# Layer c of a chain of eight layers: gate and output products in half-K pieces among heads and attention, squares on ScalarE with sums on VectorE, probabilities turned unscaled

## The chip, the core and the metric

One NeuronCore of a Trainium2 chip runs the whole program. The metric is the device time of one execution in microseconds. TensorE, VectorE, ScalarE, GpSimd and SyncE each work through their own instructions in order and meet at semaphores.

## What is computed

`x` (1 x 256 x 1024, float32) goes through eight residual layers: two of differential attention (a0, a1), a gated convolution (b), a latent attention (c), a window attention with a convolution (h), a dense feed-forward (ffn), a recurrent layer (r) and a mixture of experts (moe), in the order a0, b, c, a1, h, ffn, r, moe. The change is in c:

```python
def _mla(h, w_in, cq_g, w_uq, ckv_g, w_ukv, q_g, k_g, w_out):
    proj = h @ w_in
    c_q, c_kv, k_rope, gate = jnp.split(proj, [256, 384, 448], axis=-1)
    q = (_rms_norm(c_q, cq_g) @ w_uq).reshape(bsz, seq, 8, 192)
    kv = (_rms_norm(c_kv, ckv_g) @ w_ukv).reshape(bsz, seq, 8, 256)
    ...
    q_nope = _rms_norm(q_nope, q_g[:128])
    q_rope = _apply_rope(_rms_norm(q_rope, q_g[128:]), cos, sin)
    k_nope = _rms_norm(k_nope, k_g[:128])
    ...
    s = (qn @ kn.T + qr @ k_rope.T) * scale
    p = _chunk_causal_softmax(s, s0)
    o = p @ v
    ...
    return (o * jax.nn.silu(gate)) @ w_out
```

## The kernel before, in words

Tokens lie in two tiles of 128. Every weight matrix comes as granules of up to 128 x 2048 floats (1 MB). Each granule is split into two parts for TensorE: ScalarE writes the high part (`split`, L847), then VectorE the low part (L850), and a product is three matmuls a chunk (`three_passes`, L883 to L885). There are six raw slots and three split slots, so granule n is split only when n - 3 has been used. Where ScalarE and VectorE do this is decided by `ahead`: before a step of the order it emits the splits of all granules whose slot was used by an earlier step. A split is thus an instruction in the queue, with everything behind it waiting.

Eight PSUM banks are given out when the program is built (`plan_banks`): a ring of four short-lived ones (0 to 3) and one of four long-lived ones (4 to 7), each in the order of the steps. A step that needs a bank waits until its last user is released (semaphores `freed_0` to `freed_7`; `filled_n` is the other direction).

Layer c runs in three stages, in the order that `c_order` and `attention_order` give to all engines. *Gate stage*: low ranks of both tiles ("low"), four gate products ("gate"), and the turned low ranks ("lowturn"). *Head stage*: for each pair of heads and tile a q product (two heads of 192 columns) and a kv product (two heads of 256), ScalarE's squares with the accumulator (L2107), the inverse root on GpSimd (`inverse_root`, L1110, L1111: add eps, power), scaling and rotation by VectorE (L2186, `rope_one` L2212 to L2217 for q; L2198 for k), and transposes back (qturn, kturn), which ScalarE copies. An item is one such q or kv of one tile; there are 16. *Attention*: 16 steps (tile, head): scores, maximum (L1369), exponential (L1322), reciprocal and scaling of the probabilities (L1382, L1386), transposes ("weights", L1275), values (L1289), product with the gate (L1399), transposes ("output", L1298). Then the output product (`out_tensor`), the sum into x (L1218) and x's transposes for the next layer (`turn_x`, L1004).

The order of the head stage before:

```python
    for pair in range(5):
        for kind in ("q", "kv"):
            if pair < 4:
                order += [(kind, 2 * pair), (kind, 2 * pair + 1)]
            if pair >= 1:
                order += [("qturn" if kind == "q" else "kturn", i) for i in (2 * pair - 2, 2 * pair - 1)]
```

## Time and profile before

| | |
|---|---|
| median of 3 runs | 2138.75 us (2137.68 to 2139.63) |
| the profiled execution | 2138.28 us |
| its span, first to last instruction | 2136.5 us |
| TensorE busy | 1989.5 us (93%) |
| VectorE, ScalarE, GpSimd busy | 1588.1, 1236.1, 143.5 us |
| mean granted TensorE clock | 0.968 of 2.4 GHz |
| layer c, from its gate products to the next layer's first product | 346.2 to 479.3 us |

Times in rows are microseconds from the span's start, unless a mean is in ns. DVE is VectorE, ACT ScalarE, PE TensorE's matmuls, PEld its weight loads, POOL GpSimd. "idle before <-releaser" says how long the engine stood and what ended it. The clock is a share of 2.4 GHz, 0.5 being 1.2 GHz. Ends of matmuls are modelled and overlap the next start.

### The profile page before, as it was taken

The numbers are of one execution on the slowest core, as the hardware profiler recorded it, in microseconds if no ns is written. First come the engines' busy times: TensorE is split into PE (matmuls) and PEld (weight loads), VectorE is DVE, ScalarE is ACT, GpSimd is POOL, SyncE is SP. The second block draws the span as 40 slices with busy tenths as digits, with TensorE's granted clock in tenths as the row PEclk, the third lists the DMA queues.
The fourth block names the chain that finished last, engine by engine and source line by source line (L and its number), as shares of the span: only waits on it lengthen the run. The fifth ranks groups of instructions, "written<-read, shape, count | busy, mean of one in ns | idle before, by whom it ended". The sixth has DMA issues, their size and how long they took to land.

```text
span 2136.5 us, 26626 instructions
## 1 busy us (share of the span) xinstructions
PE 1989.5 (93%) x9460; PEld 1654.3 (77%) x9460; DVE 1588.1 (74%) x1962; ACT 1236.1 (58%) x1494; POOL 143.5 (7%) x209
## 2 busy tenths in 40 slices
PE   7988989689988799999889999999999999999998
PEld 6767868467867578887877878888888888888886
DVE  6664975558556744444678888898888889888887
ACT  5451135535554344343567767777777777777775
POOL 3013401305001000000000000000000000000000
PEclk9999999699999789999999999999999999999999
DMA  8422234205324225555147989899898989989894
GB/s 321 142 79 82 103 127 168 77 25 195 128 71 150 86 101 195 184 190 190 48 197 278 373 311 373 341 367 371 334 367 336 374 341 365 376 332 374 322 375 191
DMA packets 70518, 499.98 MB, mean 234 GB/s; under 512 B 8736, under 2 KB 8736, under 8 KB 10528
## 3 DMA queue, kind: packets, MB, share of 16 engines
q1 hardware_dynamic: 70432, 498.87, 62.4%
q8 instruction: 50, 0.82, 0.2%
q14 instruction: 36, 0.29, 0.0%
HBM read 497.79 MB, written 1.05 MB: 233 GB/s over the span
## 4 chain that ended last, share of the span: by engine, by line
PE 81%; DVE 10%; ACT 4%; issue 3%; POOL 1%; DMA 0%; DVEq 0%; SPq 0%; ACTq 0%; POOLq 0%
PE psum L883 24%; PE psum L885 23%; PE psum L884 23%; PE psum L1882 4%; DVE low L850 3%; ACT high L847 2%; PE psum L2850 2%; PE psum L2911 1%; PE psum L1890 1%; POOL small L1111 1%; PE psum L1127 1%; ACT h L1616 1%; DVE x L1218 0%; PE psum L1898 0%; DVE small L1659 0%
## 5 line engine op out<-in xcount | busy, mean ns | idle before, releaser
L850 DVE TENSOR_TENSOR low<-raw,high 128x2048 fp32r<-128x2048 f32 (+1 forms) x460 | 1046.6, 2281 | 307.2 <-ACT high L847 304.4
L847 ACT ACTIVATE high<-raw 128x2048 fp32r<-128x2048 f32 (+1 forms) x460 | 877.3, 1912 | 418.8 <-PE psum L885 395.7
L883 PE MATMUL psum<-high,yT_high 128*128 128x512 f32 x1672 | 669.6, 400 | 52.6 <-DVEq L2190 16.9
L885 PE MATMUL psum<-high,yT_low 128*128 128x512 f32 x1672 | 659.0, 394 | 0.0
L884 PE MATMUL psum<-low,yT_high 128*128 128x512 f32 x1672 | 657.5, 393 | 0.0
L883 PEld LDWEIGHTS psum<-high,yT_high 128*128 128x128 f32 x1672 | 318.6, 191 | 127.2 <-issue 37.2
L885 PEld LDWEIGHTS psum<-high,yT_low 128*128 128x128 f32 x1672 | 318.7, 191 | 68.1
L884 PEld LDWEIGHTS psum<-low,yT_high 128*128 128x128 f32 x1672 | 319.7, 191 | 62.0
L883 PE MATMUL psum<-high,hT_high 128*128 128x512 f32 (+2 forms) x560 | 220.2, 393 | 13.4 <-DVE h L1793 6.1
L885 PE MATMUL psum<-high,hT_low 128*128 128x512 f32 (+2 forms) x560 | 216.3, 386 | 0.0
L884 PE MATMUL psum<-low,hT_high 128*128 128x512 f32 (+2 forms) x560 | 216.1, 386 | 0.0
L883 PEld LDWEIGHTS psum<-high,hT_high 128*128 128x128 f32 x560 | 105.3, 188 | 38.6 <-issue 11.0
L885 PEld LDWEIGHTS psum<-high,hT_low 128*128 128x128 f32 x560 | 105.2, 188 | 21.3
L884 PEld LDWEIGHTS psum<-low,hT_high 128*128 128x128 f32 x560 | 105.4, 188 | 19.9
L1882 PE MATMUL psum<-arena,raw 128*128 128x256 f32 x384 | 83.7, 379 | 0.0
L1882 PEld LDWEIGHTS psum<-arena,raw 128*128 128x128 f32 x384 | 72.9, 190 | 9.9
L1971 DVE SCALAR_TENSOR_TENSOR arena<-arena,const 128x256 f32<-128x256 f32 x184 | 74.5, 481 | 0.4
L883 PE MATMUL psum<-hT_high,high 128*128 128x256 f32 x224 | 64.8, 290 | 4.9 <-DVE low L850 3.6
L884 PE MATMUL psum<-hT_low,high 128*128 128x256 f32 x224 | 64.0, 286 | 0.0
L885 PE MATMUL psum<-hT_high,low 128*128 128x256 f32 x224 | 64.0, 286 | 0.0
L2963 ACT ACTIVATE arena<-psum 128x512 f32<-128x512 f32 x56 | 33.5, 599 | 45.5 <-PE psum L885 45.5
L1917 ACT ACTIVATE arena<-psum,const 128x256 f32<-128x256 f32 x16 | 6.7, 470 | 78.9 <-PE psum L1882 78.9
(326 smaller groups left out, 1775.5 us busy)
## 6 DMA issues: line engine op xcount, KB each, us to landing
raw<-in_moe_weights SPq DMA_DIRECT2D x336, 1024.0 KB, 4.8
raw<-in_weights SPq DMA_DIRECT2D x132, 1024.0 KB, 5.0
raw<-in_weights SPq DMA_DIRECT2D x2, 896.0 KB, 4.6
raw<-in_weights SPq DMA_DIRECT2D x2, 768.0 KB, 4.4
x<-in_x SPq DMA_DIRECT2D x2, 512.0 KB, 4.2
raw<-in_weights SPq DMA_DIRECT2D x2, 512.0 KB, 3.6
out_x<-x SPq DMA_DIRECT2D x1, 1024.0 KB, 5.6
const<-in_constants SPq DMA_DIRECT2D x1, 512.0 KB, 8.4
```

Of the source, the lines that this page charges most:

```text
L847: eng.activation(high, raw, ACT.Copy).then_inc(k.high_ready, 1)
L850: eng.tensor_tensor(low, raw, high.bitcast(F32), ALU.subtract).then_inc(k.low_ready, 1)
L883: pe.matmul(out, lhs.high, rhs.high, start=start, stop=False)
L884: pe.matmul(out, lhs.high, rhs.low, start=False, stop=False)
L885: return pe.matmul(out, lhs.low, rhs.high, start=False, stop=stop)
L1111: pool.tensor_tensor(rstd, rstd, k.neghalf[:, 0:n], ALU.pow).then_inc(ready, 1)
L1127: last = pe.transpose(k.bank(("norm", n, i))[:, first:first + P], k.h[:, t, P * c:P * (c + 1)], k.ident)
L1616: last = act.activation(probs[:, s % 2, SEQ * m:SEQ * m + e], k.bank(name)[:, SEQ * m:SEQ * m + e], ACT.Exp, bias=low[:, m:m + 1], scale=q ...
L1882: last = pe.matmul(k.bank(name)[:, SEQ * half:SEQ * (half + 1)], w[:, c, P * half:P * (half + 1)], b.hT[:, c, :], start=(c == 0), stop=(c ...
L1971: last = v.scalar_tensor_tensor(b.conv[:, c, :], window, weight, b.conv[:, c, :], ALU.mult, ALU.add)
L2850: last = pe.matmul(k.bank(name)[:, P * (c % 4):P * (c % 4 + 1)], k.h[:, tile, P * c:P * (c + 1)], b.placed[:, tile, :], start=(tile == 0), ...
L2963: k.release(act.activation(b.silu[:, i % 2, :], k.bank(name), ACT.Silu), name)
```

## The change

All of it is in layer c. `c_order` is now written out, with eight half-K pieces of the gate product (unit, half, tile) between head products and transposes; pieces take long-lived banks. kv products come first. Squares of q and kv are plain ScalarE operations into a buffer, and VectorE sums them (`reduce`), one item ahead of the scaling (`C_REDUCE_LEAD = 1`). The rotation of q runs over both heads at once, with the root applied after it. Buffers of q and k are four deep. The attention has its own functions: probabilities are transposed unscaled, the reciprocal of the sums goes into the product of values and gate, and the output product too comes in eight half-K pieces, at steps 11, 13, 15, 19 and 20, the last three after step 22.

```diff
+    return [
+        ("low", 0), ("low", 1), gate(0, 0, 0), gate(0, 0, 1), ("lowturn", 0), ("lowturn", 1), gate(0, 1, 0),
+        ("kv", 0), ("kv", 1), ("q", 0), ("q", 1), gate(0, 1, 1), ("kv", 2), ("kv", 3), ("kturn", 0), ("kturn", 1),
+        ("q", 2), ("q", 3), gate(1, 0, 0), ("qturn", 0), ("qturn", 1), ("kv", 4), ("kv", 5), ("kturn", 2), ("kturn", 3),
...
+C_TURN_LAG, C_VALUE_LAG, C_REDUCE_LEAD = 2, 4, 1
+C_PIECES = {
+    11: [(0, 0, 0)], 13: [(1, 0, 0)], 15: [(0, 1, 0)], 19: [(0, 0, 1)], 20: [(1, 0, 1)], C_STEPS - 1: [(1, 1, 0), (0, 1, 1)],
+}
...
+    return order + [("turn_x", 0), ("turn_x", 1), ("piece", ("out", 1, 1, 1))]
...
-            for m, (first, n) in enumerate(parts):
-                last = act.activation(b.junk[:, junk:junk + n], bank[:, first:first + n],
-                                      ACT.Square, scale=float(n) ** -0.5, accum_out=k.group_ms[:, col + m:col + m + 1])
...
+                act.activation(squares[:, 0:2 * C_NOPE].rearrange("p (h n) -> p h n", h=2), heads[:, :, 0:C_NOPE], ACT.Square,
+                               scale=float(C_NOPE) ** -0.5)
...
+    def reduce(n):
+        kind, i = turns[n]
+        ahead(k, v, ("c", kind, i))
+        v.wait_ge(k.c_squares, n - 1)
+        last = v.tensor_reduce(k.group_ms[:, col:col + 2], squares[:, 0:2 * C_NOPE].rearrange("p (h n) -> p h n", h=2), AX, ALU.add)
...
+    for n in range(2, len(turns) + C_REDUCE_LEAD):
+        if n < len(turns):
+            reduce(n)
+        if n - C_REDUCE_LEAD >= 2:
+            at = n - C_REDUCE_LEAD
+            {"q": consume_q, "kv": consume_kv}[turns[at][0]](at)
...
+            steps.link(v.reciprocal(k.out_rstd[:, place:place + GROUP], k.c_sums[:, GROUP * g:GROUP * (g + 1)]))
+            for h in range(GROUP):
+                last = v.scalar_tensor_tensor(b.y[:, g % 2, cols], k.bank(name)[:, cols], k.out_rstd[:, place + h:place + h + 1],
+                                              b.gate[:, t, 512 * half + C_V * h:512 * half + C_V * (h + 1)], ALU.mult, ALU.mult)
...
+    ahead(k, v, k.banks.ticks[("c", C_STEPS - 1)])
+    add_to_x(k, v, ("c", "out", 2), 0, 1)
+    add_to_x(k, v, ("c", "out", 1), 1, 0)
```

The first place is VectorE's queue in the middle of the head stage. Before, from a split over kv 2 and kv 3 (`arena<-psum`, L2198) to the first head of q 4:

```order
L850 TENSOR_TENSOR low<-raw,high 128x2048 [waits dve_own,high_ready]
L2198 SCALAR_TENSOR_TENSOR arena<-psum,small,spread 128x128 [waits c_v_ready,filled_2,group_rstd_ready]
L2198 SCALAR_TENSOR_TENSOR arena<-psum,small,spread 128x128
L2198 SCALAR_TENSOR_TENSOR arena<-psum,small,spread 128x128 [waits freed_0,c_v_ready,filled_3,group_rstd_ready]
L2198 SCALAR_TENSOR_TENSOR arena<-psum,small,spread 128x128
L2186 SCALAR_TENSOR_TENSOR h<-psum,small,spread 128x128 [waits freed_1,filled_2,group_rstd_ready]
L2212 SCALAR_TENSOR_TENSOR h<-psum,small,arena 128x64
L2213 SCALAR_TENSOR_TENSOR h<-psum,small,arena 128x32
L2214 SCALAR_TENSOR_TENSOR h<-psum,small,arena 128x32
L2217 TENSOR_TENSOR h<-h 128x64 [waits dve_own]
L2186 SCALAR_TENSOR_TENSOR h<-psum,small,spread 128x128 [waits dve_own]
```

Now, from the sum of kv 7's squares (L2323) over the scaling of kv 6 (L2384), two splits (L907), the sums of q 4 (L2323, L2325) and the scaling of kv 7 to the sums of q 5:

```order
L2323 TENSOR_REDUCE small<-arena 128x2 [waits freed_1,c_squares]
L2384 SCALAR_TENSOR_TENSOR arena<-psum,small,spread 128x128 [waits group_rstd_ready,c_v_ready,filled_2]
L2384 SCALAR_TENSOR_TENSOR arena<-psum,small,spread 128x128
L907 TENSOR_TENSOR low<-raw,high 128x2048 [waits freed_0,high_ready]
L907 TENSOR_TENSOR low<-raw,high 128x2048 [waits high_ready]
L2323 TENSOR_REDUCE small<-arena 128x2 [waits c_squares]
L2325 TENSOR_REDUCE small<-arena 128x2
L2384 SCALAR_TENSOR_TENSOR arena<-psum,small,spread 128x128 [waits group_rstd_ready,c_v_ready,filled_3]
L2384 SCALAR_TENSOR_TENSOR arena<-psum,small,spread 128x128
L2323 TENSOR_REDUCE small<-arena 128x2 [waits freed_1,c_squares]
L2325 TENSOR_REDUCE small<-arena 128x2
```

Sums stand between the scalings, each waits for ScalarE's squares (`c_squares`), and two splits stand ahead of q 4's.

The second place is TensorE's queue at the same stage. Before, the transposes of kv 0 and kv 1 (L2075), and the product of q 4 to the first matmul of q 5's:

```order
L2075 MATMUL psum<-const,arena 128x128 [waits freed_2,c_k_staged]
L2075 MATMUL psum<-const,arena 128x128
L2075 MATMUL psum<-const,arena 128x128 [waits freed_3,c_k_staged]
L2075 MATMUL psum<-const,arena 128x128
L883 MATMUL psum<-high,yT_high 128x384 [waits low_ready,freed_0,freed_1]
L884 MATMUL psum<-low,yT_high 128x384
L885 MATMUL psum<-high,yT_low 128x384
L883 MATMUL psum<-high,yT_high 128x384
L884 MATMUL psum<-low,yT_high 128x384
L885 MATMUL psum<-high,yT_low 128x384
L883 MATMUL psum<-high,yT_high 128x384 [waits freed_1]
```

Now, the transposes of kv 0 and kv 1 (L2159), and the product of q 2 to the first matmul of q 3's:

```order
L2159 MATMUL psum<-const,arena 128x128 [waits freed_2,c_k_staged]
L2159 MATMUL psum<-const,arena 128x128
L2159 MATMUL psum<-const,arena 128x128 [waits freed_3,c_k_staged]
L2159 MATMUL psum<-const,arena 128x128
L940 MATMUL psum<-high,yT_high 128x384 [waits freed_0,low_ready]
L941 MATMUL psum<-low,yT_high 128x384
L942 MATMUL psum<-high,yT_low 128x384
L940 MATMUL psum<-high,yT_high 128x384
L941 MATMUL psum<-low,yT_high 128x384
L942 MATMUL psum<-high,yT_low 128x384
L940 MATMUL psum<-high,yT_high 128x384 [waits freed_1]
```

Before and now a pair's products take banks 0 and 1 and the transposes 2 and 3; q 2 now has the bank that kv 2 had.

The third place is VectorE's queue at the end of layer c. Before, from the split (L850) over the sums of outputs 0 and 1 and the low parts (L978) to the sums of outputs 2 and 3:

```order
L850 TENSOR_TENSOR low<-raw,high 128x2048 [waits high_ready]
L1218 TENSOR_TENSOR x<-x,psum 128x512 [waits filled_6]
L1218 TENSOR_TENSOR x<-x,psum 128x512 [waits filled_7]
L978 SCALAR_TENSOR_TENSOR hT_low<-psum,const,hT_high 128x256 [waits part_ready]
L978 SCALAR_TENSOR_TENSOR hT_low<-psum,const,hT_high 128x256
L978 SCALAR_TENSOR_TENSOR hT_low<-psum,const,hT_high 128x256 [waits part_ready]
L978 SCALAR_TENSOR_TENSOR hT_low<-psum,const,hT_high 128x256
L850 TENSOR_TENSOR low<-raw,high 128x2048 [waits high_ready] x2
L1218 TENSOR_TENSOR x<-x,psum 128x512 [waits filled_4]
L1218 TENSOR_TENSOR x<-x,psum 128x512 [waits filled_5]
```

Now, from the low part of the last transposed output (L2446):

```order
L2446 TENSOR_TENSOR yT_low<-psum,yT_high 128x4x128 [waits part_ready]
L907 TENSOR_TENSOR low<-raw,high 128x2048 [waits high_ready] x2
L1275 TENSOR_TENSOR x<-x,psum 128x512 [waits filled_6]
L1275 TENSOR_TENSOR x<-x,psum 128x512 [waits filled_4]
L1035 SCALAR_TENSOR_TENSOR hT_low<-psum,const,hT_high 128x256 [waits part_ready]
L1035 SCALAR_TENSOR_TENSOR hT_low<-psum,const,hT_high 128x256
L1035 SCALAR_TENSOR_TENSOR hT_low<-psum,const,hT_high 128x256 [waits part_ready]
L1035 SCALAR_TENSOR_TENSOR hT_low<-psum,const,hT_high 128x256
L1275 TENSOR_TENSOR x<-x,psum 128x512 [waits filled_5]
```

Both splits stand ahead of the sum of output (0,1) (`filled_4`), for which TensorE's turn_x waits; before, they stood behind what turn_x (0,1) needed.

## Rows read from the trace of the kernel before

**Rows 1.** Windows of layer c; columns: us, busy us of PE, PEld, DVE, ACT, POOL, clock, DMA.
```profile
346.20:369.00 22.80, 22.80 (x106) 18.89 (x106) 15.65 (x25) 15.35 (x30) 3.71 (x4) 1.00 0.57 212
369.00:422.70 53.70, 31.74 (x113) 24.70 (x111) 30.76 (x100) 30.61 (x134) 18.32 (x32) 0.68 0.19 65
422.70:455.20 32.50, 26.05 (x152) 20.90 (x152) 21.59 (x88) 14.29 (x53) 0.00 (x0) 0.94 0.14 56
```
**Rows 2.** Timeline of VectorE: splits, then the turned low ranks.
```profile
355.65 6.17 DVE L850 TENSOR_TENSOR low<-raw,high 128x2048 fp32r<-128x2048 f32 x3 [0.24 <-DVE h L2175]
361.73 1.64 DVE L2156 SCALAR_TENSOR_TENSOR yT_low<-psum,const,yT_high 128x128 fp32r<-128x128 f32 x6
```
**Rows 3.** Timeline of TensorE: starts of three head products.
```profile
379.36 0.69 PE L883 MATMUL psum<-high,yT_high 128*128 128x384 f32 x1 [0.34 <-DVEq L2190]
...
398.02 0.48 PE L883 MATMUL psum<-high,yT_high 128*128 128x512 f32 x1 [2.13 <-DVEq L2190]
...
405.61 0.43 PE L883 MATMUL psum<-high,yT_high 128*128 128x384 f32 x1
```
**Rows 4.** Timeline of ScalarE: first square of each of those products.
```profile
381.74 0.28 ACT L2107 ACTIVATE h<-psum 128x128 f32<-128x128 f32 x1 [1.64 <-issue]
...
398.99 0.28 ACT L2107 ACTIVATE h<-psum 128x128 f32<-128x128 f32 x1 [2.05 <-PE psum L885]
...
407.02 0.28 ACT L2107 ACTIVATE h<-psum 128x128 f32<-128x128 f32 x1
```
**Rows 5.** Groups of ScalarE instructions by line and shape, 369.0 to 422.7.
```profile
L2107 ACT ACTIVATION_READ_ACCUMULATOR h<-psum 128x1 f32 x48 | 9.7, 205 | 0.0
L2107 ACT ACTIVATE h<-psum 128x128 f32<-128x128 f32 x32 | 8.7, 275 | 22.5 <-PE psum L885 19.8 <-issue 1.6 <-ACT h L2107 0.9
L847 ACT ACTIVATE high<-raw 128x2048 fp32r<-128x2048 f32 x3 | 5.6, 1904 | 0.0
```
**Rows 6.** Group of VectorE's maxima in the attention, 422.7 to 455.2.
```profile
L1369 DVE TENSOR_REDUCE small<-psum 128x1 f32<-128x256 f32 x8 | 3.4, 425 | 0.3
```
**Rows 7.** The chain of waits: start us, us, engine, tile, line.
```profile
406.22 0.67 ACT h L2107 x6
...
407.28 1.03 POOL small L1111
...
408.34 0.35 DVE h L2186
```
**Rows 8.** Groups of VectorE instructions by line and shape, 369.0 to 422.7.
```profile
L850 DVE TENSOR_TENSOR low<-raw,high 128x2048 fp32r<-128x2048 f32 x3 | 6.8, 2291 | 0.8 <-ACT high L847 0.5 <-DVE h L2217 0.3
L2186 DVE SCALAR_TENSOR_TENSOR h<-psum,small,spread 128x128 f32<-128x128 f32 x16 | 5.6, 351 | 12.0 <-POOL small L1111 5.3 <-PE psum L2069 5.1 <-DVE h L2217 1.2
L2198 DVE SCALAR_TENSOR_TENSOR arena<-psum,small,spread 128x128 f32<-128x128 f32 x16 | 4.9, 346 | 7.1 <-PE psum L2075 4.6 <-POOL small L1111 1.8 <-DVE h L2217 0.4
L2212 DVE SCALAR_TENSOR_TENSOR h<-psum,small,arena 128x64 f32<-128x64 f32 x16 | 4.4, 276 | 0.0
```
**Rows 9.** Timeline of VectorE: the first score.
```profile
424.04 0.11 DVE L1368 MEMSET psum<- 64x64 f32 x1 [1.57 <-PE psum L1266]
```
**Rows 10.** Windows inside the head stage, columns as in rows 1.
```profile
372.70:376.70 4.00, 0.00 (x0) 0.00 (x0) 2.52 (x11) 2.45 (x15) 3.58 (x6) 0.80 0.62 209
376.70:382.00 5.30, 4.90 (x15) 4.32 (x16) 3.39 (x14) 1.30 (x10) 2.32 (x5) 0.51 0.10 40
```
**Rows 11.** Timeline of TensorE: the ninth score, then one whole step of the second tile.
```profile
432.41 0.60 PE L1265 MATMUL psum<-arena 128*128 128x256 f32 x2
...
439.95 0.60 PE L1265 MATMUL psum<-arena 128*128 128x256 f32 x2
...
441.55 0.60 PE L1298 MATMUL psum<-const,arena 128*128 128x128 f32 x4
```
**Rows 12.** Timeline of TensorE: first product of the next layer.
```profile
479.26 0.50 PE L883 MATMUL psum<-high,hT_high 128*128 128x512 f32 x1 [1.12 <-DVE low L850]
```
**Rows 13.** Timeline of VectorE: two sums of the output product.
```profile
481.32 1.28 DVE L1218 TENSOR_TENSOR x<-x,psum 128x512 f32<-128x512 f32 x2
```

More of the change, by code:

```diff
@@ L365, in a_attention, with c_all @@
                 banks.plan((layer, kind, i), parts=kind == "output")
+    def c_all(layer):
+        for kind, i in c_order() + c_attention_order():
+            if kind == "step":
+                banks.ticks[(layer, i)] = len(banks.order)
+            elif kind == "turn_x":
+                banks.plan(("norm", RAW_NORM[layer], i), parts=True)
+            elif kind == "piece":
+                if i[2] == 0:
+                    banks.plan(piece_name(layer, i), Banks.LONG)
+                if i[3] == 1:
+                    banks.ticks[(layer,) + i[0:3]] = len(banks.order)
+            elif kind == "values":
+                if i % GROUP == 0:
+                    banks.plan((layer, "values", i // GROUP), Banks.LONG)
+            else:
+                banks.plan((layer, kind, i), parts=kind in ("lowturn", "output"))
     def out(layer):
@@ L387, in plan_banks @@
     norm(2)
-    in_order("c", c_order(), ("lowturn",))
-    attention("c")
-    out("c")
+    c_all("c")
     norm(3)
@@ L625, in __init__ @@
         self.ratio = small(2)
+        self.c_sums = small(ITEMS)
         self.sink_exp = small(4)
@@ L1263, in attention_tensor @@
             bank = k.bank(name)
-            if kind == "c":
-                pe.matmul(bank[:, 0:e], b.qT[:, head, tile], b.kT[:, head, 0:e], start=True, stop=False)
-                last = pe.matmul(bank[:, 0:e], b.qropeT[:, head // 2, tile], b.kropeT[:, head % 2, 0:e], start=False, stop=True)
             if kind == "h":
@@ L2044, in c_tensor @@
         name = ("c", kind, i)
+        if kind == "piece":
+            c_piece(k, pe, i)
+            continue
         bank = k.bank(name)
-        if kind == "low":
-            if i == 0:
-                products(k, pe, [name, ("c", kind, 1)], g, k.hT, KC, C_HEAD_IN)
-        if kind == "gate" and i % 2 == 0:
-            products(k, pe, [name, ("c", kind, i + 1)], g + 2 + i, k.hT, KC, 512)
+        if kind == "low" and i == 0:
+            products(k, pe, [name, ("c", kind, 1)], g, k.hT, KC, C_HEAD_IN)
         if kind == "lowturn":
@@ L2085, in c_scalar @@
     act.wait_ge(k.cleared, 2)
-    squares = GROUP_MS["c"]
-    steps = k.engine_steps["act"]
+    n = 0
     for kind, i in c_order():
+        if kind == "piece":
+            _, u, half, t = i
+            if half == 1:
+                name = piece_name("c", i)
+                ahead(k, act, name)
+                k.wait_filled(act, name)
+                k.release(act.activation(b.gate[:, t, 512 * u:512 * (u + 1)], k.bank(name), ACT.Silu,
+                                         scale=token_scale(k, act, 2, t)), name)
+            continue
         name = ("c", kind, i)
@@ new lines, in low_turned @@
+    def low_turned(i):
+        name = ("c", "lowturn", i)
+        bank, tile = k.bank(name), slice(P * i, P * (i + 1))
+        k.wait_part(v, name)
+        for c in range(3):
+            gain = k.column("c_cq_norm_g", c) if c < 2 else k.column("c_ckv_norm_g", 0)
+            last = v.scalar_tensor_tensor(b.lowT.low[:, c, tile], bank[:, P * c:P * (c + 1)], gain,
+                                          b.lowT.high[:, c, tile].bitcast(F32), ALU.mult, ALU.subtract)
+        k.release(last, name)
@@ new lines, in consume_kv @@
+    def consume_kv(n):
+        _, i = turns[n]
+        name, kk, root = ("c", "kv", i), b.k[:, i % 4, :], roots(n, 2)
+        bank = k.bank(name)
+        if i >= 4:
+            k.wait_filled(v, ("c", "kturn", i - 4))
+        v.wait_ge(k.c_v_ready, i + 1)
+        v.wait_ge(k.group_rstd_ready, base + n + 1)
+        for m in range(2):
+            last = v.scalar_tensor_tensor(kk[:, P * m:P * (m + 1)], bank[:, 256 * m:256 * m + C_NOPE], root[:, m:m + 1],
+                                          k.wide("c_k_norm_g", 0, C_NOPE), ALU.mult, ALU.mult)
+        k.release(last, name)
+        k.wait_released(v, name)
+        v.sem_inc(k.c_k_staged, 1)
@@ new lines, in c_vector @@
+    for i in range(2):
+        ahead(k, v, ("c", "low", i))
+    for i in range(2):
+        consume_low(i)
+    for i in range(2):
+        ahead(k, v, ("c", "lowturn", i))
+        low_turned(i)
+    for n in range(2, len(turns) + C_REDUCE_LEAD):
[4 more added lines that the diff above has]
+            {"q": consume_q, "kv": consume_kv}[turns[at][0]](at)
+    ahead(k, v, ("c", "scores", 0))
+    c_attention_vector(k, v, b)
@@ L2200, in c_vector @@
             k.release(last, name)
             k.wait_released(v, name)
-            v.sem_inc(k.c_k_staged, 1)
-        v.sem_inc(k.c_roots_used, 1)
-    ahead(k, v, ("c", "scores", 0))
-    attention_vector(k, v, "c", b)
+            v.sem_inc(k.staged, 1)
+        g = (s - C_OUTPUT_STEP - 1) // GROUP
+        if s >= C_OUTPUT_STEP + 1 and (s - C_OUTPUT_STEP - 1) % GROUP == 0:
+            t, half = g // 2, g % 2
+            name = ("c", "output", g)
+            k.wait_part(v, name)
+            chunks, tile = slice(GROUP * half, GROUP * (half + 1)), slice(P * t, P * (t + 1))
+            k.release(v.tensor_tensor(k.yT.low[:, chunks, tile], k.bank(name).rearrange("p (c q) -> p c q", c=GROUP),
+                                      k.yT.high[:, chunks, tile].bitcast(F32), ALU.subtract), name)
```

347 lines of the change are left out of this document (247 added, 100 removed).

## Prediction

> **What bounds the kernel now.** I read the page first: TensorE is busy for nearly all of the span, so only a stage in which it stands can give something back. Then the windows of layer c, the only layer that is rewritten [rows 1]. The gate stage (346.2 to 369.0) has no hole: 22.8 us of 22.8. The head stage (369.0 to 422.7) has TensorE busy 31.7 of 53.7 us, and at a mean clock of 0.68, so it is work for little more than 20 us at the full clock. The attention (422.7 to 455.2) has it busy 26.1 of 32.5 us. What the change can win lies in the head stage and in the 6 us of the attention.
>
> Next, what paces the head stage. The chain of waits goes round a loop: product, squares on ScalarE, root on GpSimd, scaling and rotation on VectorE, and back, because VectorE frees the bank that the next product takes [rows 7]. No engine is full: VectorE and ScalarE are each busy 31 of 53.7 us [rows 1]. It is latency round that loop that costs, and this is what I weigh the change by.
>
> **The change, part by part.** The sum is made against the profiled execution, 2138.28 us (span 2136.5 and 1.8 around it); the median of the runs is 0.5 us above it.
>
> *Start of the head products.* Two gate products leave the stretch ahead of them. VectorE now splits two granules instead of three before it takes the turned low ranks: 1.7 + 2.2 us instead of the 6.1 from 355.65 to 361.73, then the same 1.6 us [rows 2]. The first product (kv 0) starts at 361.4 where q 0 started at 369.0: **7.6 us earlier**. This is the whole of what hiding the gate can give; the other five pieces (12 matmuls of 0.228 us, 2.7 us each, from 22.8 us for 96 of them and 8 transposes [rows 1]) lie among the heads.
>
> *Cost of one item.* From a product's start to ScalarE's first square: q 1.41 us at the full clock (405.61 to 407.02) and 2.38 at half (379.36 to 381.74), kv 0.97 [rows 3, 4]. Squares: the four squares of a q (0.275 us each, every one with a read of the accumulator, 0.205 [rows 5]) become two instructions, 0.56 us, and of a kv one, 0.39. The sums become VectorE's: a reduction of 256 columns, bounded below by 0.28 (a 64-column operation [rows 8]) and near 0.42, the maximum over as many [rows 6]; I take 0.42, and 0.62 for q, which has a second, shorter one that overlaps. Root: 1.45 us from the last square (406.89) to VectorE's start (408.34), 1.03 of it the power [rows 7]; unchanged. Scaling: q until its bank is free is three operations of the rotation and two of 128 columns, 1.26 us at the spacing of 0.19 and 0.27 at which such operations run (0.276 and 0.351 us each, overlapped [rows 8]), and 0.7 more for sum and scaling of the rotation; kv two of 0.346, 0.61 together. From a freed bank to the product 0.14 us. So VectorE does 2.6 us for a q, against 2.3 before (two rotations, 408.34 to about 410.6), and 1.0 for a kv against 0.6. ScalarE is relieved, VectorE is loaded.
>
> *The loop.* After the first four items every head product alternates between banks 0 and 1, and VectorE's order is: reduce item n+1, scale n, reduce n+2, scale n+1. Product n+2 needs the bank of n. So between "scale n" and "reduce n+2" VectorE stands for the product and the squares. One item costs 0.14 + 1.41 + 0.56 + 0.05 + 0.62 + 1.26 = **4.0 us for a q** and 0.14 + 0.97 + 0.39 + 0.05 + 0.42 + 0.61 = **2.6 for a kv**. The root is hidden, but the loop through the bank is not. Before, the stage took 53.7 us for 16 items, 3.4 each; the mean of 4.0 and 2.6 is 3.3, so the loop as such is no shorter.
>
> *Splits inside the loop.* VectorE's queue now holds the split of a granule ahead of four reductions, each waiting for ScalarE's half (1.90, then 2.29 us, 2.2 in a row [rows 5, 8]). The first: gate piece (0,1,1) ends 6.2 us after kv 0 starts, silu and split end at 9.0, VectorE's at 11.2; then reduce 0.42, scale q 1 1.96, reduce 0.42, scale kv 2 0.61: kv 2 frees its bank at 14.6. Behind kv 6 two splits stand together, 5.5 us of them uncovered.
>
> *Sum of the stage at the full clock:* 14.6; kv 3 3.4; q 2 4.0; q 3 4.0 (short split and a gate piece included); kv 4 2.6; kv 5 3.8 (1.2 us of a piece ahead of kv 6's product); kv 6 2.6; kv 7 6.7; q 4 to q 6 12.1; q 7 2.6; and 6.5 until VectorE reaches the first score, since two more splits and ScalarE's last turned heads and table load stand there: 62.9 us. From 361.4 that is 424.3, where the first score's memset now starts at 424.04 [rows 9]: **+0.3 us**. The head start is spent on the longer loop.
>
> *Clock.* After 4 us without a matmul (372.7 to 376.7) the granted clock was 0.51 over the next 5.3 us, the 1.2 GHz level [rows 10]. In the new order TensorE stands 5 us before the transposes of kv 1 and 5 us before q 5, and between q 5, q 6 and q 7 for more than half the time. I take q 2, q 3, q 5, q 6, q 7 at half clock: 5 x 0.97 = **+5.0**, and three gate pieces that follow such holes at half of the 1.2 us that each may lose before the clock comes back: **+1.8**. The Trainium skill says as much (TensorE: Matmul & The Clock Gate, "A second HAM failure mode: psum-queue depth-cycling"): a kernel that goes through its psum banks with small pauses keeps falling back to half rate. By that rule the term would be all of it, 8.6 instead of 6.8; the same page's general rule, that activity releases the throttle, would favour the change and make it 0, which is the second rival.
>
> *Attention, first tile.* Normalizing moves from the probabilities to the values: two VectorE operations a step go. But eight steps take only 8.4 us now (424.04 to 432.41 [rows 9, 11]), and TensorE's matmuls, ScalarE's exponential, read and copy, and the loop over two banks of scores keep a step near 1.05 us: **0**. The clock is low at its start, since TensorE rests through the two splits ahead of it, for longer than before: **+0.8**, an estimate between 0 and the 1.6 us that two more steps at half clock would cost.
>
> *Second tile and output.* One step is 1.6 us of TensorE (439.95 to 441.55 [rows 11]). TensorE's work from the ninth score on is 12.8 for eight steps, 1.2 for transposes and products that lag into them, 1.8 for the outputs' transposes, 21.9 for eight pieces, 0.9 for turning x (8 transposes, at the 0.11 us that a quarter of a 512-column matmul and its start make): 38.6. Waits: 1.0 where the first four scalings of y (0.35 us each [rows 8]) stand ahead of a maximum; 1.3 where piece (1,1,0) waits for its granule; and 5.7 at the end. There turn_x waits for the sum of output (0,1), which stands on VectorE behind the split of a granule that ScalarE can begin only when piece (0,1,1) is done: 0.3 + 1.9 + 2.2 + 2 x 0.6 + 0.1 [rows 5, 8, 13]. Total 46.6 us. Before, 432.41 to 479.26 [rows 11, 12] is 46.9: **−0.2**. What the attention's holes give, the end takes. After 5.7 us of rest the clock is low again for turn_x (+0.8), most of the last piece (+2.0) and the next layer's first matmuls (+0.4): **+3.2**.
>
> Sum: 0.3 + 5.0 + 1.8 + 0.8 − 0.2 + 3.2 = **+10.9 us**, 2149 us.
>
> **Rivals.** *The loops are covered, and work decides (27%).* If the products really run ahead, the stage ends with VectorE's work: from 361.4, 8 x 1.0 + 8 x 2.6 + 12.7 of splits (five of 2.2, one of 1.7) = 41.5 us, the first score at 404, 20 us earlier. With 4 us lost at the end that is 2122; halfway, 2130. For it: TensorE has half the stage free. Against it: banks 0 and 1 are taken in turn. It decides as soon as the reduction of item n+2 starts within 1 us of the scaling of item n.
> *The clock holds (18%).* Same loops, but the pieces keep TensorE at 2.4 GHz: 0.3 + 0 − 0.2 = +0.1 us, 2138. For it: busy time in the stage rises by five pieces. Against: the holes are 5 us long, and 4 us sufficed [rows 10].
> *All pieces slow (inside "slower").* Gate pieces and the next layer's start at half clock throughout: 5 us more, 2154.
>
> **How the numbers follow.** Forecast with its slow end 55% (2143 to 2156), clock holds 18% (2134.5 to 2142.5), work decides 27% (2114 to 2134). 0.2% is 4.3 us, about what a measurement tells from no change. Leaving out the lower half of the fast case and the slow end's tip gives 2126 to 2156. Faster 0.27, same 0.18, slower 0.55; the likeliest case alone has 2143 to 2156.
>
> **What would show it.** Right: the first score's memset 63 to 73 us after kv 0; VectorE idle 1.5 to 3 us ahead of each reduction from q 2 on, released by ScalarE's squares; q products at 0.32 us spacing; a hole of 5 to 6 us ahead of the last turn_x, released by VectorE; layer c's windows longer although TensorE's holes in the gate are gone. Wrong: the first score before 420, reductions that follow scalings at once, or a clock of 1.00 throughout.

## The result, and the profile after the change

| | before | after |
|---|---|---|
| median | 2139.05 us (2137.68 to 2140.17, 6 runs) | 2146.23 us (2144.62 to 2147.36, 6 runs) |
| the profiled execution, its span | 2138.28, 2136.5 us | 2146.32, 2144.5 us |
| TensorE busy | 1989.5 us | 1993.5 us |
| mean granted TensorE clock | 0.968 | 0.966 |
| first head product (kv 0; before q 0) | 369.0 | 361.44 |
| first score's memset on VectorE | 424.04 | 430.03 |
| ninth score | 432.41 | 438.16 |
| next layer's first product | 479.26 | 489.13 |

The change makes the kernel slower: ratio 1.0034, 95% interval 1.0024 to 1.0043. The forecast was 2149. Ahead of layer c the two traces stand 0.35 us apart, which is in the differences below.

Windows of layer c in the changed kernel, to be held against [rows 1]: the start of the layer, the head stage, eight steps of the first tile, then all up to the next layer's first product.

```profile
core 0: us, PE busy (x) PEld busy (x) DVE busy (x) ACT busy (x) POOL busy (x), PEclk, DMA share, GB/s
361.40:430.03 68.63, 45.44 (x184) 37.03 (x184) 37.19 (x103) 29.08 (x67) 17.63 (x32) 0.78 0.26 93
430.03:438.16 8.13, 6.96 (x34) 6.70 (x35) 4.01 (x22) 4.38 (x19) 0.00 (x0) 0.58 0.42 144
438.16:489.13 50.97, 42.51 (x212) 34.84 (x211) 24.09 (x60) 20.39 (x47) 0.00 (x0) 0.93 0.19 63
```

TensorE works longer in the head stage than before (45.4 of 68.6 us, against 31.7 of 53.7), but the stage begins 7.6 us earlier and ends 6.0 us later. No engine fills it. Where VectorE stands is seen in its groups of the head stage (the last part is the idle time just ahead of the group, and what ended it):

```profile
L907 DVE TENSOR_TENSOR low<-raw,high 128x2048 fp32r<-128x2048 f32 (+1 forms) x6 | 13.1, 2201 | 6.9 <-ACT high L904 6.9
L2323 DVE TENSOR_REDUCE small<-arena 128x2 f32<-128x256 f32 x16 | 6.7, 419 | 23.5 <-ACT arena L2249 13.9 <-ACT arena L2253 9.3
L2384 DVE SCALAR_TENSOR_TENSOR arena<-psum,small,spread 128x128 f32<-128x128 f32 x16 | 4.8, 343 | 0.5 <-POOL small L1168 0.5
```

23.5 of its 31 idle us stand ahead of the new reductions (L2323), ended by ScalarE's squares of a q (L2249, 13.9 us, all of it ahead of the five q below) or of a kv (L2253, 9.3 us, of which kv 6 has 4.51 and kv 7 1.49); the root (L1168) ends next to nothing. Another 6.9 us stand ahead of splits. In time, the reductions of q 2, q 3, q 5, q 6, q 7, and the end of the stage:

```profile
378.46 0.42 DVE L2323 TENSOR_REDUCE small<-arena 128x2 f32<-128x256 f32 x1 [3.03 <-ACT arena L2249]
382.56 0.42 DVE L2323 TENSOR_REDUCE small<-arena 128x2 f32<-128x256 f32 x1 [2.96 <-ACT arena L2249]
...
408.29 0.42 DVE L2323 TENSOR_REDUCE small<-arena 128x2 f32<-128x256 f32 x1 [2.96 <-ACT arena L2249]
412.91 0.42 DVE L2323 TENSOR_REDUCE small<-arena 128x2 f32<-128x256 f32 x1 [2.50 <-ACT arena L2249]
417.46 0.42 DVE L2323 TENSOR_REDUCE small<-arena 128x2 f32<-128x256 f32 x1 [2.44 <-ACT arena L2249]
...
423.88 2.29 DVE L907 TENSOR_TENSOR low<-raw,high 128x2048 fp32r<-128x2048 f32 x1 [2.67 <-ACT high L904]
427.73 2.29 DVE L907 TENSOR_TENSOR low<-raw,high 128x2048 fp32r<-128x2048 f32 x1 [1.56 <-ACT high L904]
430.03 0.11 DVE L2415 MEMSET psum<- 64x64 f32 x1
```

The products between them, on TensorE (q 5's first two matmuls, then those of q 7): each waits for VectorE to free a bank, and they follow each other at 0.32 us instead of 0.17. Before q 5, VectorE makes two splits (4.5 us) ahead of the scaling that frees its bank.

```profile
405.38 0.69 PE L940 MATMUL psum<-high,yT_high 128*128 128x384 f32 x1 [5.29 <-DVE arena L2384]
405.86 0.53 PE L941 MATMUL psum<-low,yT_high 128*128 128x384 f32 x1
...
414.55 0.69 PE L940 MATMUL psum<-high,yT_high 128*128 128x384 f32 x1 [2.27 <-DVE h L2369]
415.04 0.52 PE L941 MATMUL psum<-low,yT_high 128*128 128x384 f32 x1
```

The end of the layer, on VectorE (a split, then the sums of outputs 2 and 1), and what it does to TensorE:

```profile
479.03 2.29 DVE L907 TENSOR_TENSOR low<-raw,high 128x2048 fp32r<-128x2048 f32 x1 [4.21 <-ACT high L904]
481.24 1.28 DVE L1275 TENSOR_TENSOR x<-x,psum 128x512 f32<-128x512 f32 x2
```

```profile
482.66 1.94 PE L1061 MATMUL psum<-const,x 128*128 128x128 f32 x8 [5.61 <-DVE x L1275]
484.26 0.78 PE L940 MATMUL psum<-high,yT_high 128*128 128x512 f32 x1
484.83 0.63 PE L941 MATMUL psum<-low,yT_high 128*128 128x512 f32 x1
```

The pieces for the two sums had been done since 477.1, before VectorE took up the split; x could be turned only behind it, after 5.61 us of rest.

Two theories go into the experiments. **Mine:** the head stage is paced by a loop through the bank (item n+2's product needs the bank of item n), in which product and squares are exposed; TensorE's half clock makes it longer; and the end is lost to the order on VectorE. **The rivals:** ScalarE's and VectorE's queues (splits, silu, turned heads) or the root pace the stage whatever the banks, and the clock is only a companion of the holes.

### The profile page after: what moved, and what is told of

The parts are those of the page before. It is cut to its first block, busy times and chain, and to the rows that moved or that the text cites. A ratio compares the mean times of both kernels' runs of the same rounds, so it can differ in the third digit from the quotient of the medians.

```text
span 2144.5 us, 26519 instructions
## 1 busy us (share of the span) xinstructions
PE 1993.5 (93%) x9460; PEld 1659.7 (77%) x9460; DVE 1586.1 (74%) x1946; ACT 1231.2 (57%) x1422; POOL 138.0 (6%) x209
## 4 chain that ended last, share of the span: by engine, by line
PE 82%; DVE 9%; ACT 4%; issue 3%; POOL 1%; DMA 0%; DVEq 0%; SPq 0%; ACTq 0%; POOLq 0%
PE psum L940 24%; PE psum L942 23%; PE psum L941 23%; PE psum L1937 4%; DVE low L907 3%; ACT high L904 2%; PE psum L3101 2%; PE psum L3162 1%; PE psum L1945 1%; POOL small L1168 1%; PE psum L1184 1%; ACT h L1671 1%; DVE x L1275 0%; PE psum L1061 0%; PE psum L1953 0%
## 5 line engine op out<-in xcount | busy, mean ns | idle before, releaser
L907 DVE TENSOR_TENSOR low<-raw,high 128x2048 fp32r<-128x2048 f32 (+1 forms) x460 | 1046.8, 2280 | 306.5 <-ACT high L904 305.3
L940 PE MATMUL psum<-high,yT_high 128*128 128x512 f32 (+1 forms) x1672 | 668.9, 400 | 51.2 <-issue 14.4
L942 PE MATMUL psum<-high,yT_low 128*128 128x512 f32 (+1 forms) x1672 | 658.0, 394 | 0.0
L941 PE MATMUL psum<-low,yT_high 128*128 128x512 f32 (+1 forms) x1672 | 656.5, 393 | 0.0
L940 PE MATMUL psum<-high,hT_high 128*128 128x512 f32 (+2 forms) x560 | 222.9, 398 | 11.1 <-DVE h L1848 6.1
```

What stands on the lines that cost most here:

```text
L907: eng.tensor_tensor(low, raw, high.bitcast(F32), ALU.subtract).then_inc(k.low_ready, 1)
L940: pe.matmul(out, lhs.high, rhs.high, start=start, stop=False)
L941: pe.matmul(out, lhs.high, rhs.low, start=False, stop=False)
L942: return pe.matmul(out, lhs.low, rhs.high, start=False, stop=stop)
```

## The experiments

### 1. The order at the end of the layer

```diff
-    ahead(k, v, k.banks.ticks[("c", C_STEPS - 1)])
+    ahead(k, v, k.banks.ticks[("c", "out", 0, 1)] - 1)
     add_to_x(k, v, ("c", "out", 2), 0, 1)
     add_to_x(k, v, ("c", "out", 1), 1, 0)
     low_parts(k, v, RAW_NORM["c"], (0, 1))
+    ahead(k, v, k.banks.ticks[("c", C_STEPS - 1)])
```

> Only VectorE's order at the end of layer c changes: the low split of the next layer's granule stands behind the two sums and the low parts of the turned x, not ahead of them. My theory: the hole of 5.61 us ahead of the last turn_x is that split; it shrinks to 1.5 us or less, and as the clock then holds, the turned x and the last piece run at 0.228 us a matmul. The next layer's first product comes 5 to 7 us earlier, and the program takes 2139.5 to 2141.5 us. Rival: the next layer's first product then waits for the later split (2.2 us plus ScalarE's high parts), and 2 us or less of it is left: 2144 or more.

Measured: 2138.05 us (median of 11), a little better than expected; ratio to the kernel before 0.9994 (0.9985 to 1.0003), where the change alone has 1.0034. The same place on TensorE:

```profile
478.49 1.06 PE L1061 MATMUL psum<-const,x 128*128 128x128 f32 x8 [0.87 <-DVE x L1275]
479.31 0.48 PE L940 MATMUL psum<-high,yT_high 128*128 128x512 f32 x1
...
482.14 0.39 PE L940 MATMUL psum<-high,hT_high 128*128 128x512 f32 x1
```

The hole ahead of the transposes is 0.87 us instead of 5.61, the eight transposes take 1.06 instead of 1.94, and the next layer begins at 482.14 instead of 489.13, although this execution stood 0.6 us behind the other just before (the piece that starts at 471.33 in the change starts here at 471.91). So 7.6 us are gained: 4.7 of the hole and 2.9 of the clock behind it. The order of one split against two sums is worth about as much as the whole change costs.

### 2. The reduction right before its item

```diff
-C_TURN_LAG, C_VALUE_LAG, C_REDUCE_LEAD = 2, 4, 1
+C_TURN_LAG, C_VALUE_LAG, C_REDUCE_LEAD = 2, 4, 0
```

> VectorE reduces item n just before it scales item n, not one item ahead. So the root's 1.45 us stands in VectorE's queue in every item, but the product of item n+1 and its squares run beside it. Theory of the bank loop: a q costs 0.62 + 1.45 + 1.96 = 4.0 us whatever the clock of the products, a kv 2.5; the five q at half clock lose their 0.97 each: head stage 3 to 6 us shorter, 2140 to 2143 us. Rival: the reduction ahead pays for itself, the root comes on top of the wait for the product; 16 x 1.45 us more with 5 off is 2160 or more.

Measured: 2145.33 us, ratio 1.0028 (1.0018 to 1.0038): hardly faster than the change, neither my 2140 to 2143 nor the rival's 2160. Two items of the last pair on VectorE, in the timeline:

```profile
413.52 0.41 DVE L2323 TENSOR_REDUCE small<-arena 128x2 f32<-128x256 f32 x1
...
415.65 0.29 DVE L2363 TENSOR_TENSOR h<-psum,arena 128x128 f32<-128x128 f32 x1 [1.53 <-POOL small L1168]
...
417.16 0.41 DVE L2323 TENSOR_REDUCE small<-arena 128x2 f32<-128x256 f32 x1
```

The wait for the squares is gone and the root's 1.53 us stands in its place. A q now costs 3.64 us at whatever clock, against 4.6 in the last items of the change. But the first score comes at 428.67, only 1.4 us earlier (2.3 us, counted from kv 0, which starts at 362.38 here), since the early items, which had no wait for a bank, now pay for the root too: the scaling of q 0 begins at 370.65 where the change had it at 367.29 (0.9 us of that stood ahead of the stage). So the wait for product and squares can be covered by a later reduction, at the root's price; with two banks one of the two waits was paid in either order.

### 3. Four banks for the head products

The order of every engine stays; the banks are given by name, and each bank counts its own uses.

```diff
+C_BANKS = {
+    ("kv", 0): 0, ("kv", 1): 1, ("q", 0): 2, ("q", 1): 3, ("kv", 2): 6, ("kv", 3): 7, ("q", 2): 0, ("q", 3): 1, ("kv", 4): 6,
+    ("kv", 5): 7, ("kv", 6): 0, ("kv", 7): 1, ("q", 4): 6, ("q", 5): 7, ("q", 6): 0, ("q", 7): 1,
+}
+C_BANKS.update({(kind, i): 2 + i % 2 for kind in ("qturn", "kturn") for i in range(8)})
...
-                banks.plan((layer, kind, i), parts=kind in ("lowturn", "output"))
+                banks.plan((layer, kind, i), parts=kind in ("lowturn", "output"), bank=C_BANKS.get((kind, i)))
```

> Same order of all engines; only the banks of the head products change: they go round four banks (0, 1, 6, 7), the turned heads round 2 and 3. Theory of the bank loop: VectorE's idle time ahead of the reductions of q2, q3, q5, q6, q7 (3.03, 2.96, 2.96, 2.50, 2.44 us, released by ScalarE's squares) is the wait for a bank; it falls below 0.7 each, and the holes of TensorE ahead of q3, q6, q7 go. The stage from kv0 to the first score falls from 68.6 us by 8 to 12, the program to 2134.5 to 2138.5 us. Rival: ScalarE's queue (splits, silu, turned heads ahead of the squares) sets those waits; the idle time stays, and the program is at 2144 to 2147.

Measured: 2129.14 us, ratio 0.9955 (0.9941 to 0.9968), 17 us below the change and 10 below the kernel before. VectorE's groups and the stage's window:

```profile
L914 DVE TENSOR_TENSOR low<-raw,high 128x2048 fp32r<-128x2048 f32 (+1 forms) x6 | 13.1, 2199 | 4.8 <-ACT high L911 4.8
L2330 DVE TENSOR_REDUCE small<-arena 128x2 f32<-128x256 f32 x16 | 6.7, 416 | 7.4 <-ACT arena L2260 4.0 <-ACT arena L2256 2.8
```

```profile
361.40:411.48 50.08, 37.05 (x185) 31.30 (x183) 36.98 (x103) 29.73 (x67) 17.64 (x32) 0.93 0.36 125
```

The idle time ahead of the reductions falls from 23.5 to 7.4 us, the clock rises from 0.78 to 0.93, and the first score comes at 411.48, 18.5 us earlier. I had expected 8 to 12, since I had counted only the five q. Their waits fall by 11.1 us (q 2 still waits 1.98 and q 3 0.79, against an expected 0.7 or less), the kv's by 5.3 (kv 6 from 4.51 to 1.78, kv 7 from 1.49 to nothing), those of the splits by 2.1. Ahead of kv 6 it was not the bank itself: in the change its product starts at 394.00, right behind a gate piece that TensorE took up only at 389.58, after kv 5 had waited for its bank, and that ran mostly at half clock. With the order on ScalarE and VectorE unchanged, the queues cannot have set the waits that went; the 4.8 us ahead of the splits and what is left of kv 6's wait are not the loop's.

### 4 and 5. Filling TensorE's holes

Additional 128x512 matmuls into a gate bank that is free, their result not used. In the first attempt they were placed by the steps of the order:

```diff
+        if (kind, i) in C_EXTRA:
+            ...
+            for _ in range(C_EXTRA[(kind, i)]):
+                pe.matmul(k.bank(at), k.hT.high[:, 0, 0:P], right, start=True, stop=True)
```

> 44 additional 128x512 matmuls (one pass, result not used) stand in TensorE's holes: 14 ahead of the turned kv1, 4 ahead of q3, 14 ahead of q5, 5 ahead of q6, 7 ahead of q7. Theory of the clock: q2, q3, q5, q6, q7 then run at 0.16 us a matmul, not 0.32 to 0.38, VectorE's idle time ahead of their reductions shrinks by about 0.97 each, and the first score comes 3 to 5 us earlier: 2141 to 2143.5 us. Rival: the clock is no part of the loop's price, or the matmuls stand in the way: 2146 or more.

Measured: 2147.95 us, ratio 1.0039 (1.0025 to 1.0053). The placement missed: the step "q 4" issues the products of q 4 and q 5, so the 14 matmuls meant to stand ahead of q 5 stood behind it. q 5 stayed at half clock, as did q 3 for the same reason, and q 6 came late (VectorE idle 4.71 us ahead of its reduction instead of 2.50). Only q 7 tells something: at the full clock its reduction waited 1.48 us instead of 2.44. In the second attempt they stand between the two products of a pair:

```diff
+C_EXTRA = {
+    ("c", "kturn", 0): 14, ("c", "kturn", 1): 4, ("c", "q", 2): 7, ("c", "q", 4): 20, ("c", "kturn", 5): 5, ("c", "q", 6): 9,
+}
```

> Additional 128x512 matmuls (result not used) as before, but now placed where TensorE stands: 14 and 4 around the turned kv1, 7 between q2 and q3, 20 between q4 and q5, 5 behind the turned kv5, 9 between q6 and q7. Theory of the clock: the products behind them run at 0.16 to 0.18 us a matmul, VectorE's idle time ahead of the reductions of q3, q5, q6, q7 falls by 0.9 us each (q2 by 0.5), and the program is 3.5 to 4.5 us shorter than the changed kernel: 2141.5 to 2143. Rival: the products gain, but the fillings stand in front of them: 2145 to 2148.

Measured: 2140.96 us, ratio 1.0004 (0.9995 to 1.0013): 5.3 us less than the change by the medians, more than expected. VectorE ahead of q 3, q 5, q 6, q 7:

```profile
381.10 0.42 DVE L2340 TENSOR_REDUCE small<-arena 128x2 f32<-128x256 f32 x1 [1.99 <-ACT arena L2266]
...
405.38 0.42 DVE L2340 TENSOR_REDUCE small<-arena 128x2 f32<-128x256 f32 x1 [2.01 <-ACT arena L2266]
409.02 0.42 DVE L2340 TENSOR_REDUCE small<-arena 128x2 f32<-128x256 f32 x1 [1.52 <-ACT arena L2266]
412.60 0.42 DVE L2340 TENSOR_REDUCE small<-arena 128x2 f32<-128x256 f32 x1 [1.46 <-ACT arena L2266]
```

Each waits 0.95 to 0.98 us less, and so does q 2 (2.07 instead of 3.03). The stage takes 62.2 us (first head product 361.90, first score 424.10) instead of 68.6, at a granted clock of 0.97 instead of 0.78. So the half clock costs 6.4 us here: by the times at which VectorE ends each scaling, 4.9 on the five q and 1.5 on gate pieces. The loop stays, at the full clock, as long as it was worked out to be in sum.

### 6. The same banks in the kernel before

```diff
         for kind, i in order:
-            banks.plan((layer, kind, i), parts=kind in parts)
+            bank = {"q": 4, "kv": 6}[kind] + i % 2 if layer == "c" and kind in ("q", "kv") else None
+            banks.plan((layer, kind, i), parts=kind in parts, bank=bank)
```

> The kernel before the change, with nothing but the banks of its head products changed: q in 4 and 5, kv in 6 and 7, the turned heads round 0 to 3. Theory of the bank loop: there too an item paid for product, squares, root and scaling in a row because the product two items on needs its bank; with four banks, product, squares and root run ahead while VectorE scales, and the stage of 53.7 us falls to 40 to 44: 2125 to 2130 us. Rival: the root in VectorE's path or the two staging buffers set the pace: 2136 to 2140.

Measured: 2128.58 us, ratio 0.995 (0.9936 to 0.9963); first score at 410.95, 13.1 us earlier than in the kernel before. From q 0 to the first score it takes 41.95 us instead of 55.04:

```profile
369.00:410.95 41.95, 25.68 (x123) 20.89 (x122) 30.68 (x100) 30.32 (x134) 20.50 (x32) 0.86 0.26 82
```

The old kernel was held by the same two banks. With four, old and changed kernel are level (2128.58 and 2129.14).

### 7 and 8. The mends together

Run 7 has the edits of 1 and 3. Run 8 also puts off three splits, by giving the granules whose slots they need a later step (`step` is what `ahead` compares):

```diff
             in_piece(a, layer, "gate", 1, 0, C_HEAD_IN + 512)
+            granules[-1].step = banks.ticks[(layer, 7)] - 1
             whole(w["c_w_uq"][0], 4 * C_QK, 4 * C_QK, (layer, "q", 7))
+            granules[-1].step = banks.ticks[(layer, 9)] - 1
             in_piece(a, layer, "gate", 1, 1, C_HEAD_IN + 512)
+            granules[-1].step = banks.ticks[(layer, 12)] - 1
```

> The four product banks and VectorE's order at the end of the layer together. They lie in different stages, so their gains should add: 17 us of the banks and 8 of the end, 2120 to 2122 us. Rival: the end's gain shrinks, because with the earlier attention the granules land too late: 2124 or more.

> As the run before, and the splits of the first three output granules are put off: they stand behind attention steps 7, 9 and 12 instead of behind kv6 and ahead of the first score. Theory: the first score comes 5 to 8 us earlier (2.3 + 2.8 + 2.3 us stand ahead of it with the banks alone, and 2.2 behind kv6), and ScalarE and VectorE have room for them in the second tile's steps, which TensorE paces: 2114 to 2118 us. Rival: the splits delay the exponentials and maxima there and give back what they took: 2119 to 2122.

Measured: run 7 2121.99 us, ratio 0.9921 (0.9907 to 0.9935); run 8 2116.98 us, ratio 0.9898 (0.9882 to 0.9913). The gains of 1 and 3 add (8.2 and 17.1 us, together 24.2), as expected for different stages. In run 8 the first score comes at 403.70, behind the heads and no longer behind a split:

```profile
403.70 0.11 DVE L2425 MEMSET psum<- 64x64 f32 x1 [1.76 <-PE psum L2191]
```

That is 6.8 us earlier than in run 7 (410.49), of which the medians keep 5.0. This version beats both kernels: 22 us below the one before.

### 9 to 11. What hiding is worth

Run 9 is the change with all gate pieces ahead of the heads and their granules moved to match, run 11 the same with the edits of 1 and 3, run 10 the change with the output pieces behind the last step (the splits and the sum that hang on them move too).

```diff
-        ("low", 0), ("low", 1), gate(0, 0, 0), gate(0, 0, 1), ("lowturn", 0), ("lowturn", 1), gate(0, 1, 0),
-        ("kv", 0), ("kv", 1), ("q", 0), ("q", 1), gate(0, 1, 1), ("kv", 2), ("kv", 3), ("kturn", 0), ("kturn", 1),
...
+        ("low", 0), ("low", 1), gate(0, 0, 0), gate(0, 0, 1), ("lowturn", 0), ("lowturn", 1), gate(0, 1, 0), gate(0, 1, 1),
+        gate(1, 0, 0), gate(1, 0, 1), gate(1, 1, 0), gate(1, 1, 1),
+        ("kv", 0), ("kv", 1), ("q", 0), ("q", 1), ("kv", 2), ("kv", 3), ("kturn", 0), ("kturn", 1),
...
```

```diff
-    11: [(0, 0, 0)], 13: [(1, 0, 0)], 15: [(0, 1, 0)], 19: [(0, 0, 1)], 20: [(1, 0, 1)], C_STEPS - 1: [(1, 1, 0), (0, 1, 1)],
+    C_STEPS - 1: [(0, 0, 0), (0, 0, 1), (1, 0, 0), (1, 0, 1), (0, 1, 0), (1, 1, 0), (0, 1, 1)],
```

> The changed kernel with all eight gate pieces ahead of the head products again (granules in the same order), everything else as changed. The first head product comes 7.6 us later; in exchange no piece and no split of a gate granule stands in the loop, which takes 8 x 4.0 + 8 x 2.6 = 52.8 us, 5 for the clock, about 2.2 behind kv7 and 4 ahead of the first score. My estimate from the prediction's own terms: first score near 433, program 2147 to 2150, so that hiding the gate is worth 1 to 4 us and not 7.6. Rivals: all 7.6 us are lost (2152 to 2155), or the splits in the loop cost as much as they hide (2144 to 2146).

> The changed kernel with all output pieces behind the last attention step, as before the change. In the second tile TensorE's work sets the step (1.6 us), so the pieces hide little there; holes come back only where the last values wait for sums and turned outputs: 1 to 4 us slower than the changed kernel, 2147 to 2150. Rival: the pieces fill real holes, and 5 of them (13.7 us) outside cost 8 or more: 2154.

> All gate pieces ahead of the heads, together with the four product banks and the mended end. With product, squares and root covered, VectorE's work sets the head stage: 8 x 2.6 + 8 x 1.0 + three splits of 2.3 = 36 us and some 3 of waits, from 369.0: first score near 408, where it is 410.5 with the pieces among the heads. So hiding the gate is worth nothing while a split stands in VectorE's queue: 2119 to 2123 us. Rival: the 7.6 us of the later start stay: 2127 to 2130.

Measured: run 9 2150.82 us, ratio 1.0059 (1.0046 to 1.0073); run 10 2148.16, ratio 1.0045 (1.0031 to 1.0059); run 11 2123.22, ratio 0.993 (0.9917 to 0.9944).

Run 9 is 0.25% slower than the change, 4.6 us by the medians and a little more than the expected 1 to 4, and not by the way expected. The first head product does not start at 369.0:

```profile
380.26 0.76 PE L941 MATMUL psum<-high,yT_high 128*128 128x512 f32 x1 [5.11 <-DVE low L908]
```

TensorE waits for the split of kv's granule, which gets its slot only when a gate piece has been used. So the heads begin 18.8 us later than in the change, and yet the first score (436.62) comes only 6.6 later: the stage from kv 0 on takes 56.4 us instead of 68.6, since no piece and three splits instead of six stand in its loop, and this although the granted clock in it is lower (0.59 instead of 0.78). Of the 18.8 us by which the change starts its heads earlier than this run, 12.2 are paid back in the loop.

Run 11 against run 7 leaves it open what hiding is worth with four banks. The heads take about what was worked out (38.2 us; 39 expected), but they start at 377.65, not at 369.0, behind the same wait for kv's split, and the first score is 5.4 us later than run 7's (415.86 to 410.49), the next layer's first product 5.0 (466.19 to 461.21). The medians are only 1.2 us apart and the ratios 0.0009, less than either interval. Part of the difference is in the layer behind, of which more below: the same 24 matmuls take 6.60 us in run 11's trace and 8.17 in run 7's. So this order of granules loses about 5 us in layer c, and no run has all pieces ahead of the heads with the heads starting at 369.0.

Run 10 differs from the change by 0.0011, again inside the intervals. From the ninth score to the next layer's first product it takes 51.96 us where the change takes 50.97: the five output pieces among the steps (13.7 us of work) hide about 1.0 us, as TensorE has little room there. Behind the last step the seven pieces took 19.3 us without a hole, and then the hole ahead of turn_x was 6.21 us.

## Why the prediction was right, and where not

**The start.** Worked out 361.4, measured 361.44.

**The loop of the head stage.** The step was "the loop through the bank is not hidden; 62.9 us at the full clock". Run 5 is the test that keeps the order and takes the low clock away: 62.2 us. Run 3 takes the bank away: 50.2 us from kv 0 (361.32) to the first score. The reductions of the five q named waited 2.4 to 3.0 us each for ScalarE's squares, as forecast (1.5 to 3); those of the kv did not keep to that range (0.63, 0.95, 4.51 and 1.49 us for kv 4 to kv 7). The closeness of the sum is in part luck, as errors in its terms cancel. In run 5, by the times at which VectorE ends each scaling, q 4 to q 6 took 10.8 us (12.1 worked out) and q 7 1.6 (2.6), but kv 5 5.0 (3.8), and from q 7 to the first score it was 8.3 (6.5): a q cost 3.6 us and not 4.0, and the gate pieces and the last two splits cost more. The prediction names the same loop in the kernel before and finds it "no shorter"; what I did not draw from this is that more banks cure both kernels, which run 6 shows.

**The clock in the heads.** The step was +5.0 for five q and +1.8 for gate pieces, 6.8; run 5 gives 6.4. Exactly the five q named ran at half clock, 0.97 us each, and the pieces cost the stage 1.5. The 1.2 us that each piece may lose stood in no row: by their rows the three took 3.3, 4.4 and 4.5 us where 2.7 is the full clock, so they lost 0.5, 1.7 and 1.8 us of their own time, and that the stage paid only part of it makes the term's fit luck. By the Trainium skill's rule (TensorE: Matmul & The Clock Gate, "A second HAM failure mode: psum-queue depth-cycling") I had put 8.6; the trace agrees in kind, as products behind a wait for a bank ran at half clock, though not all of them: q 4, behind holes of 1.44 and 0.88 us, ran at the full clock. The size was nearer the sum from the rows. Stage as a whole: forecast 69.7 us, measured 68.6.

**The first tile.** This step was mis-sized, and not in the clock. Forecast were 0 for the two VectorE operations that go and +0.8 us for the clock; eight steps took 8.13 us against 8.37 before, so −0.2. The low clock did cost its time. In the change the steps at half clock take 1.5 us (scores at 434.22, 435.71, 437.21), TensorE has no listed hole between them and VectorE waits for its scores; the next one, mostly at the full clock, takes 0.95:

```profile
435.36 0.11 DVE L2415 MEMSET psum<- 64x64 f32 x1 [0.87 <-PE psum L2181]
...
435.71 0.64 PE L2180 MATMUL psum<-arena 128*128 128x128 f32 x2
...
437.21 0.52 PE L2180 MATMUL psum<-arena 128*128 128x128 f32 x2
...
438.16 0.67 PE L2180 MATMUL psum<-arena 128*128 128x256 f32 x2
```

The windows of the same eight steps before, in run 10 and in run 9, the last two with the change's code for them:

```profile
424.04:432.41 8.37, 7.61 (x45) 6.03 (x45) 6.67 (x37) 4.09 (x20) 0.00 (x0) 0.87 0.39 147
430.95:438.17 7.22, 5.87 (x34) 5.24 (x35) 4.23 (x24) 4.38 (x19) 0.00 (x0) 0.76 0.49 168
436.62:443.53 6.91, 5.46 (x42) 4.70 (x41) 4.36 (x24) 5.30 (x20) 0.00 (x0) 1.00 0.46 153
```

So the clock (0.58 in the change) costs 0.9 to 1.2 us, about the forecast 0.8, and the term put at 0 is the one that failed: VectorE is busy 4.0 us instead of 6.7, and at higher clocks the steps take 6.9 to 7.2 us instead of 8.4. The new attention gains 1.2 to 1.5 us in the first tile, and in the change the low clock takes most of it back. No run separates the two operations from the rest of the new attention. (Run 8, also at 1.00, takes 7.69 us, with a table load of 1.28 us on ScalarE between its first score and its first exponential.)

**Second tile and end.** The hole ahead of turn_x was forecast at 5.7 us and measured at 5.61. The stretch from the ninth score to the next layer's first product grew by 4.1 us (from 46.85 to 50.97). Up to that product the terms were −0.2 and +2.8, so +2.6; the 0.4 for the next layer's first matmuls would fall behind it, and it did not come (they follow each other at 0.23 us, the full clock). Run 1 shows hole and clock together to be worth 7.6 us, 2.9 of it the clock, as worked out. TensorE's listed holes in the stretch sum to 8.2 us (0.79, 0.52, 1.26 and 5.61), with 8.0 worked out. What is left of the 1.5 us, some 1.3, is TensorE's own work, summed up at 38.6, and pauses too short to be listed.

**The sum.** Worked out at the next layer's first product: 0.3 + 6.8 + 0.8 − 0.2 + 3.2 = 10.9; measured 9.9, of which 0.35 stood ahead of the layer. The parts missed by more than that and cancel: heads and first tile came out 1.1 and 1.0 us below the forecast, the rest 1.1 above it. Of the 9.9 us the program keeps 8.0 (2146.32 to 2138.28). The prediction had no term for that, and this is the larger part of its miss of 2.8 us. Matched matmul by matmul, the two traces come nearer to each other by 0.7 us where the next layer turns the last of x (TensorE had a hole of 0.43 us there before, at 482.75, and has none now), and by 1.3 in that layer's attention, where 24 matmuls that are the same in every version took 7.93 us before and 6.60 now:

```profile
599.72:607.64 7.92, 5.53 (x24) 4.27 (x24) 6.17 (x13) 3.00 (x9) 0.00 (x0) 0.78 0.40 134
608.81:615.41 6.60, 4.21 (x25) 3.25 (x25) 5.09 (x9) 2.05 (x6) 0.00 (x0) 1.00 0.46 158
```

This place takes between 6.6 and 8.2 us in the traces of the thirteen versions. What decides there over the clock is not known, and a comparison of two versions by one trace each can be off by as much.

**The rivals.** "Work decides" forecast a first score at 404 and 2122 us if the products really ran ahead. They did not. With four banks they do for the most part, and with all six splits in place the first score still came at 411.5 (run 3) and 410.5 (run 7). The 403.7 of run 8 comes with three of the splits put off, so it matches 404 only by luck. The rival counted 28.8 us of VectorE's work outside the splits where run 3 has 23.9 (37.0 busy, 13.1 of it splits), and no waits where run 3 has 13 us of them. "The clock holds" (2138) is what run 5 made true for the heads: 2141.

## What to carry to other kernels

When several engines hand work round in a pipeline, write down which PSUM bank each step takes before reading anything into busy shares: products that take two banks in turn made a loop here out of all that stands between them, and moving work from one engine to another within that loop did not shorten it, while two more banks gave 17 us, and 10.5 in the kernel before. With four banks the two kernels are level (2129.14 and 2128.58 us). Work hidden inside such a loop brings its own instructions along on the other engines (here splits and silu), and they are paid there (12.2 of 18.8 us in run 9); what it hides must be weighed against those. Where an in-order queue has both a long job that nobody needs yet and a short one that another engine stands waiting for, their order alone can be worth more than a rewritten stage (8.2 us in run 1).
